# Last units of two products by column halves, and sixteen modulation columns moved

## The chip, the cores and the metric

One NeuronCore of one Trainium2 chip runs the program. The metric is the device time of one execution in microseconds (us); all times here are in us unless marked ns.

## The reference

512 tokens of 1024 channels pass through a first block (a short gated convolution, then a squared-ReLU MLP, both with modulation by a vector c) and through two layers of a second block. What matters for the change is the first block and the step into the second:

```python
mod_lat = [m[:, None, :] for m in jnp.split(jax.nn.silu(c) @ ada_w[i] + ada_b[i], N_MOD, axis=-1)]
g_pre, g_post, g_pre_ff, g_post_ff = norm_gains[i]
a_lat = modulate(rmsnorm(h_lat, g_pre), mod_lat[0], mod_lat[1])
y_lat = short_gated_conv(a_lat, sc_w_in[j], sc_conv[j], sc_w_out[j])
h_lat = h_lat + mod_lat[2] * rmsnorm(y_lat, g_post)
f_lat = squared_relu_mlp(modulate(rmsnorm(h_lat, g_pre_ff), mod_lat[3], mod_lat[4]), mlp_w_in[i], mlp_w_out[i])
h_lat = h_lat + mod_lat[5] * rmsnorm(f_lat, g_post_ff)
...
h = rms_norm(x, even_norm_g[i])
x = x + even_mixer(h, even_w_in[i], ...)
```

An rmsnorm divides each token by the root of its mean square over the 1024 channels.

## The kernel before

**Tiling.** Activations are kept with channels on the partitions: 8 chunks of 128 channels by 512 tokens (X, Y, XH, HH and so on). A matrix product is cut into units of 256 output columns. For a unit, SyncE loads the weights into RAW, ScalarE rounds them to a high half WH (hi_half), VectorE subtracts to get the low half WL (lo_half), and TensorE does three matmuls (high by high, high by low, low by high) for each of 8 chunks of input and each of 2 halves of output, 48 in all. The two output chunks go to PSUM banks 2j and 2j+1, with j = unit % 2. `product` (line 1844) does both halves inside its loop over the input chunks, so both banks are complete only at the unit's end (semaphore s_mm).

**Units.** 0 to 11 are the gated convolution's input product, 12 to 15 its output product, 16 to 47 the MLP (four groups of four units in and four units out), from 48 on the second block.

**Border 1, after unit 15.** The output Y has to be normalised, scaled, added to X, and X normalised again before unit 16 can start. To save a pass over X, the mean square of the new X is put together from three sums over channels: of Y squared (bank S1), of the gated Y squared (S2) and of the cross product 2·gate·Y·X (S3). The loop over units 12 to 15 (VectorE at lines 1427 to 1443, ScalarE at 817 to 826) copies the two chunks of a unit out of PSUM (L1431), makes cross products (L1438), squares (L688) and gated squares (L826), and adds the squares of units 12 to 14 up in SQ (L1163). GpSimd (POOL, lines 566 to 578) adds the cross products and gated squares of chunks 0 to 5 into SQ3 and SQ2. VectorE adds the last pair of each itself (L1445, L1447). TensorE sums over channels with matmuls on a matrix of ones, which are fp32 and appear in the trace as two passes each: last_squares (L1922), SQ2 (L2079), SQ3 (L2082), two_squares (L1928), the last cross products (L2085) and the last gated squares (L2087). Behind them stand the sixteen columns of the MLP's modulation (mod_columns, L1955): one column of PSUM for 128 rows of the modulation, a matmul with 128 weights columns and one moving column, again two passes each; and keep_busy (L1909), matmuls whose result nobody reads. ScalarE takes Ln and Exp of the first sum into R (L696, L698). VectorE then works out the second mean square in four operations (L1464, L1467, L1469, L1472), ScalarE takes its root into SQ (L831, L833), and VectorE and ScalarE make X, its scaled form (L1459), shift it (L703), round it to XH (L706) and subtract to XL (L1485) chunk by chunk. VectorE adds the bias to the columns at L1478 and L1480 in between. Units 16 and 17 are multiplied together, chunk by chunk (two_units).

**Border 2, after unit 47.** The same with one norm fewer: residual_window (L1278) adds the last output chunks to Y, ScalarE squares them, TensorE sums SQ (L1922), three columns, the last two squares (L1928), five columns and three keep_busy matmuls; R follows at L696, and post_norm feeds unit 48.

**What sets the order.** Every engine runs its instructions in the order written, and semaphores tie them. Each POOL addition waits for its product and for the addition before it; cross_product(n) and gated_square(n) have two buffers each, chosen by n % 2.

Of the kernel before, what the change touches and what calls it, by code (L numbers as in the profile page):

```python
# [22 lines left out]
ALU = mybir.AluOpType  # L23
# [4 lines left out]
P = 128  # L28
# [133 lines left out]
def program(nc, i, out):  # L162
    ctx = ExitStack()
    with ctx:
# [5 lines left out]
        def sem(name):  # L170
            return ctx.enter_context(nc.semaphore(name))
# [114 lines left out]
        s_pn, e_g = sem("postnorm_scaled"), sem("logit_scaled")  # L286
        c_z, c_t, c_y, c_g, c_h = (sem("gconv_" + x) for x in ("cv", "centre", "taps", "gated", "hi"))
        m_r, m_f, m_h = (sem("mlp_" + x) for x in ("relu", "squared", "hi"))
# [251 lines left out]
        def _(pool):  # L540
# [24 lines left out]

            for n in range(1, 6):
                pool.wait_ge(x_p, n + 1)
                if n == 1:
                    pool.tensor_tensor(SQ3, cross_product(0), cross_product(1), ALU.add).then_inc(x_sp, 1)
                else:  # L570
                    pool.wait_ge(x_sp, n - 1)
                    pool.tensor_tensor(SQ3, SQ3, cross_product(n), ALU.add).then_inc(x_sp, 1)
                pool.wait_ge(x_q, n + 1)
                if n == 1:
                    pool.tensor_tensor(SQ2, gated_square(0), gated_square(1), ALU.add).then_inc(x_sq, 1)
                else:
                    pool.wait_ge(x_sq, n - 1)
                    pool.tensor_tensor(SQ2, SQ2, gated_square(n), ALU.add).then_inc(x_sq, 1)
# [87 lines left out]
        def _(act):  # L666
# [147 lines left out]
            act.activation(PS_[:, S0_BANK, :], PS_[:, S0_BANK, :], ACT.Exp, scale=-2.0).then_inc(s_ms, 1)  # L814
            for u in range(12, 16):
                if u < 15:
                    hi_half(u + 2, u % 2, 0)
                    hi_half(u + 2, u % 2, 1)
                for c in range(2):
# [323 lines left out]
        def _(dve):  # L1143
# [282 lines left out]
            dve.tensor_scalar(sc_(S_2MG0, 8), sc_(S_MG0, 8), 2.0, None, ALU.mult).then_inc(s_sm, 1)  # L1426
            for u in range(12, 16):
                n0, j, last = 2 * (u - 12), u % 2, u == 15
                dve.wait_ge(s_mm, u + 1)
# [9 lines left out]
                if not last:  # L1439
                    lo_half(u + 2, j, 0)  # L1440
                    lo_half(u + 2, j, 1)
                    add_square(ST_Y0, n0)
                    add_square(ST_Y0, n0 + 1)
# [78 lines left out]
            clear_sum(ST_Y1)  # L1522
            for u in range(U_MLP + 28, U_MLP + 32):
                residual_window(u, u % 2, 2 * (u - U_MLP - 28), ST_Y1, Y)
            post_norm(ST_Y1, 1, S_MG1, "even_norm")
            prep_late(U_EVEN + 1)
# [316 lines left out]
        def _(pe):  # L1843
# [230 lines left out]
            mod_columns(16, 24)  # L2074
            for u in range(12, 16):
                product(u, u % 2, HH, HL, 8, s_h, 0)
            last_squares(ST_Y0, S1_BANK)
            pe.wait_ge(x_sq, 5)
            pe.matmul(PS_[:, S2_BANK, :], ONES[:, :], SQ2, start=True, stop=False)  # L2079
            pe.wait_ge(x_sp, 5)  # L2080
            pe.wait_ge(s_ev, 15)
            pe.matmul(PS_[:, S3_BANK, :], ONES[:, :], SQ3, start=True, stop=False)  # L2082
            two_squares(ST_Y0, S1_BANK)
            pe.wait_ge(x_pair, 1)
            pe.matmul(PS_[:, S3_BANK, :], ONES[:, :], cross_product(6), start=False, stop=True).then_inc(x_23, 1)  # L2085
            pe.wait_ge(x_pair, 2)
            pe.matmul(PS_[:, S2_BANK, :], ONES[:, :], gated_square(6), start=False, stop=True).then_inc(x_23, 1)  # L2087
            pe.wait_ge(s_ad, 16)
            pe.wait_ge(s_sm, 15)
            pe.wait_ge(s_ev, 16)  # L2090
            keep_busy(1, 2)
            mod_columns(24, 32, last=False)
            keep_busy(1, 2)
            mod_columns(32, 40)
            keep_busy(2, 2)
            for g in range(4):
# [422 lines left out]
```

## Time and profile before

| | |
|---|---|
| three runs | 1703.54, 1704.07, 1704.09; median 1704.07 |
| the profiled execution | 1704.55 |
| its span, first to last instruction | 1702.8 |
| TensorE busy | 1685.1 (99% of the span), 7761 matmul records |
| VectorE, ScalarE, GpSimd busy | 1095.9, 692.2, 163.3 |
| mean granted TensorE clock | 0.998 |
| window 213.35 to 232.30 (border 1) | TensorE busy 18.95, granted clock 0.82 |
| window 577 to 600 (border 2) | TensorE busy 21.98, granted clock 1.00 |

The profiled execution's own time is 1.75 above its span. Busy time of TensorE counts keep_busy too, and matmuls overlap in their records: two in a row start 0.227 apart where each shows 0.39.

### The profile page before, as it was taken

To read this page: it belongs to the slowest core of one execution; us is meant where nothing else is said; L and a number is where in the kernel's file an instruction comes from. 1 tells how busy PE (TensorE), PEld (TensorE's weight loads), DVE (VectorE), ACT (ScalarE), POOL (GpSimd) and SP (SyncE) were. 2 spreads that over 40 slices of the span, in tenths; PEclk is the share of its full clock that TensorE was granted. 3 is DMA by queue.
4 is the path that set the end of the run, shared out by engine and by line. 5 is a ranking of instruction groups with operands and counts; after the bars stand their busy time and mean duration, and the time that the engine had idled before them with its cause. 6 is when DMAs were issued, how large, how long until landed. Compare 5 with 4: busy or idle time off the path is not lost.

```text
span 1702.8 us, 21701 instructions
## 1 busy us (share of the span) xinstructions
PE 1685.1 (99%) x7761; PEld 1378.7 (81%) x7761; DVE 1095.9 (64%) x1680; ACT 692.2 (41%) x992; POOL 163.3 (10%) x160
## 2 busy tenths in 40 slices
PE   8999999999999999999999999999999999999999
PEld 7888878888888778888888888888756888888888
DVE  7799885353535586755664664769998666366374
ACT  4322353232323346644432432447666443243243
POOL 1000400000000042100000000005881000000000
PEclk9999999999999999999999999999999999999999
DMA  8676314333332133503323322232211323323222
GB/s 280 219 236 220 129 57 131 99 99 99 117 99 93 56 86 106 134 26 99 123 99 99 123 99 85 78 85 55 70 50 50 99 99 99 99 98 99 79 82 87
DMA packets 184994, 180.46 MB, mean 106 GB/s; under 512 B 3888, under 2 KB 182324, under 8 KB 184924
## 3 DMA queue, kind: packets, MB, share of 16 engines
q1 hardware_dynamic: 184924, 179.54, 33.1%
q8 instruction: 43, 0.70, 0.2%
q14 instruction: 27, 0.22, 0.0%
HBM read 173.15 MB, written 2.10 MB: 103 GB/s over the span
## 4 chain that ended last, share of the span: by engine, by line
PE 88%; DVE 7%; issue 2%; POOL 1%; ACT 1%; DMA 0%; DVEq 0%; POOLq 0%; SPq 0%; ACTq 0%
PE PSUM L1857 23%; PE PSUM L1858 23%; PE PSUM L1859 23%; DVE PSUM L1789 3%; POOL CP L635 1%; PE PSUM L2238 1%; DVE WL L1150 1%; PE PSUM L2270 1%; PE PSUM L2269 1%; PE PSUM L1890 1%; PE PSUM L1891 1%; PE PSUM L1889 1%; PE PSUM L2271 1%; PE PSUM L2303 1%; PE PSUM L2304 1%
## 5 line engine op out<-in xcount | busy, mean ns | idle before, releaser
L675 ACT ACTIVATE WH<-RAW 128x1024 fp32r<-128x1024 f32 x266 | 273.6, 1053 | 711.4 <-PE PSUM L1859 673.0
L1857 PE MATMUL PSUM<-XH,WH 128*128 128x512 f32 x1152 | 449.5, 390 | 0.0
L1858 PE MATMUL PSUM<-XL,WH 128*128 128x512 f32 x1152 | 448.2, 389 | 0.0
L1859 PE MATMUL PSUM<-XH,WL 128*128 128x512 f32 x1152 | 448.2, 389 | 0.0
L1150 DVE TENSOR_TENSOR WL<-RAW,WH 128x1024 fp32r<-128x1024 f32 x270 | 331.0, 1248 | 7.9 <-ACT WH L675 7.7
L1857 PEld LDWEIGHTS PSUM<-XH,WH 128*128 128x128 f32 x1152 | 216.2, 188 | 45.4 <-issue 0.7
L1858 PEld LDWEIGHTS PSUM<-XL,WH 128*128 128x128 f32 x1152 | 216.2, 188 | 45.4 <-issue 0.7
L1859 PEld LDWEIGHTS PSUM<-XH,WL 128*128 128x128 f32 x1152 | 216.2, 188 | 45.2
L1857 PE MATMUL PSUM<-HH,WH 128*128 128x512 f32 x632 | 246.6, 390 | 0.4
L1859 PE MATMUL PSUM<-HH,WL 128*128 128x512 f32 x632 | 246.0, 389 | 0.0
L1858 PE MATMUL PSUM<-HL,WH 128*128 128x512 f32 x632 | 245.9, 389 | 0.0
L1671 DVE TENSOR_TENSOR ZP<-PSUM,R 128x512 f32<-128x512 f32 x88 | 56.7, 687 | 172.1 <-PE PSUM L1859 172.1
L1857 PEld LDWEIGHTS PSUM<-HH,WH 128*128 128x128 f32 x632 | 118.6, 188 | 27.0 <-DVE HL L1695 2.1
L1859 PEld LDWEIGHTS PSUM<-HH,WL 128*128 128x128 f32 x632 | 118.6, 188 | 24.8
L1858 PEld LDWEIGHTS PSUM<-HL,WH 128*128 128x128 f32 x632 | 118.6, 188 | 24.4
L1278 DVE TENSOR_TENSOR X<-PSUM,X 128x512 f32 (+1 forms) x60 | 38.6, 686 | 141.7 <-PE PSUM L1859 110.9
L635 POOL TENSOR_TENSOR CP<-CP,PRD 128x512 f32<-128x512 f32 x67 | 86.3, 1289 | 451.2 <-ACT PRD L1101 431.7
L1682 DVE SCALAR_TENSOR_TENSOR TA<-ZP,VCOL,TA 128x512 f32<-128x512 f32 x176 | 120.2, 747 | 0.0
L1789 DVE SCALAR_TENSOR_TENSOR PSUM<-UPAD,VCOL,PSUM 128x512 f32<-128x512 f32 x123 | 83.4, 749 | 0.4
L1185 DVE SCALAR_TENSOR_TENSOR MACC<-ARAW,small,MACC 128x256 f32<-128x256 f32 x140 | 70.5, 504 | 5.0
L1504 DVE TENSOR_SCALAR TA<-PSUM 128x512 f32<-128x512 f32 x32 | 20.6, 686 | 80.3 <-PE PSUM L1859 78.4
L994 ACT ACTIVATE TA<-ZP,VCOL 128x512 f32<-128x512 f32 x88 | 66.4, 802 | 0.0
(401 smaller groups left out, 2062.4 us busy)
## 6 DMA issues: line engine op xcount, KB each, us to landing
RAW<-in_ffn_w_up SPq DMA_DIRECT2D x44, 1024.0 KB, 5.1
ARAW<-in_ada_w SPq DMA_DIRECT2D x24, 1024.0 KB, 5.3
RAW<-in_mlp_w_in SPq DMA_DIRECT2D x16, 1024.0 KB, 5.3
RAW<-in_mlp_w_out SPq DMA_DIRECT2D x16, 1024.0 KB, 4.9
RAW<-in_ffn_w_down SPq DMA_DIRECT2D x16, 1024.0 KB, 5.0
RAW<-in_sc_w_in SPq DMA_DIRECT2D x9, 1024.0 KB, 5.1
RAW<-in_even_w_in SPq DMA_DIRECT2D x8, 1024.0 KB, 5.6
RAW<-in_ffn_w_down SPq DMA_DIRECT2D x8, 768.0 KB, 4.4
```

The lines of the kernel that those rows point to most:

```text
L635: pool.tensor_tensor(CP[:, n, :], CP[:, n, :], PRD[:, before % RING, :], ALU.add).then_inc(g_a, 1)
L675: act.activation(WH[:, j, a:b, :], RAW[:, j, a:b, :], ACT.Copy).then_inc(s_hi, 1)
L994: act.activation(TA[:, c, :], ZP[:, c, 2:T + 2], ACT.Identity, scale=col(f"fw{layer}2", it * 2 + (half + 2 * first + c)), bias=col(f"fb{la ...
L1150: tt(WL[:, j, a:b, :], RAW[:, j, a:b, :], WH[:, j, a:b, :].bitcast(F32), ALU.subtract).then_inc(s_lo, 1)
L1185: stt(dst, w, s, dst, ALU.mult, ALU.add).then_inc(s_as if k < 7 else s_ad, 1)
L1278: ins = dve.tensor_copy(d, src) if first else tt(d, src, d, ALU.add)
L1671: tt(ZP[:, c, 2:T + 2], banks(j, c), R[:, :], ALU.mult).then_inc(f_z, 1)
L1682: stt(TA[:, c, :], ZP[:, c, tap:tap + T], col(f"fw{layer}{tap}", it * 2 + (half + 2 * first + c)), TA[:, c, :], ALU.mult, ALU.add).then_in ...
L1789: stt(acc, src, w, acc, ALU.mult, ALU.add).then_inc(g_v, 1)
L1857: pe.matmul(o, wh, mh[:, k, :], start=(k == 0), stop=False)
L1858: pe.matmul(o, wh, ml[:, k, :], start=False, stop=False)
L1859: mm = pe.matmul(o, wl, mh[:, k, :], start=False, stop=(k == kn - 1))
```

## The change

At both borders the last unit is multiplied by output halves: all 24 matmuls of the first half, a semaphore, then all 24 of the second. VectorE takes chunk 6 out after the first and chunk 7 after the second, and adds the square of chunk 6 to SQ in between; TensorE then sums SQ and the square of chunk 7 only. At border 1, GpSimd also adds chunk 6's cross product and gated square, VectorE's two pair additions are gone, and the last sums take chunk 7 alone. The sixteen modulation columns move from border 1 to behind units 12 and 13, eight each, and VectorE's two small operations on them to a place in front of chunk 6. VectorE's v1 waits for one of the two last sums rather than both. keep_busy is six in a row at border 1 (before: one, one, two) and two at border 2 (before: three). ScalarE's rounding of the first half of unit 17's weights stands between its work for chunk 6 and chunk 7.

```diff
@@ gpsimd
-            for n in range(1, 6):
+            for n in range(1, 7):
                 pool.wait_ge(x_p, n + 1)
@@ scalar
-            for u in range(12, 16):
-                if u < 15:
-                    hi_half(u + 2, u % 2, 0)
-                    hi_half(u + 2, u % 2, 1)
+            for u in range(12, 15):
+                hi_half(u + 2, u % 2, 0)
+                hi_half(u + 2, u % 2, 1)
...
+            square(ST_Y0, 6, Y[:, 6, :])
+            gate(6)
             hi_half(U_MLP + 1, 1, 0)
+            square(ST_Y0, 7, Y[:, 7, :])
+            gate(7)
             rms(ST_Y0, 1.0 / D, S1_BANK)
@@ vector
-            dve.wait_ge(x_p, 8)
-            tt(cross_product(6), cross_product(6), cross_product(7), ALU.add).then_inc(x_pair, 1)
-            dve.wait_ge(x_q, 8)
-            tt(gated_square(6), gated_square(6), gated_square(7), ALU.add).then_inc(x_pair, 1)
+            def last_chunk(n):
+                dve.tensor_copy(Y[:, n, :], banks(1, n % 2)).then_inc(s_xu, 1)
+                dve.wait_ge(s_xu, 8 * ST_Y0 + n + 1)
+                if n == 7:
+                    dve.tensor_copy(sc_(S_DUMP), sc_(S_EPS)).then_inc(s_ev, 1)
+                dve.wait_ge(x_sp, n - 2)
+                stt(cross_product(n), Y[:, n, :], sc_(S_2MG0 + n), X[:, n, :], ALU.mult, ALU.mult).then_inc(x_p, 1)
+            dve.wait_ge(s_ac, 6)
+            tt(sc_(S_MOD + 24, 16), PS_[:, COL_BANK, 24:40], col("ada_b", 24, 16), ALU.add).then_inc(s_sm, 1)
+            dve.wait_ge(s_sm, 18)
+            stt(sc_(S_GS1, 8), sc_(S_MOD + 32, 8), 1.0, col("gains", 16, 8), ALU.add, ALU.mult).then_inc(s_sm, 1)
+            dve.wait_ge(t_mm, T_MM + 1)
+            last_chunk(6)
+            dve.wait_ge(s_sqr, squares_before(ST_Y0) + 7)
+            dve.wait_ge(s_sqa, sum_steps(ST_Y0) + 7)
+            tt(SQ[:, :], SQ[:, :], TF[:, 0, :], ALU.add).then_inc(t_sqa, 1)
+            dve.wait_ge(s_mm, 16)
+            last_chunk(7)
             lo_half(U_MLP + 1, 1, 0)
...
             dve.wait_ge(s_r, ST_Y0 + 1)
+            dve.wait_ge(x_23, 1)
+            tt(v, PS_[:, S2_BANK, :], R[:, :], ALU.mult).then_inc(x_v, 1)
             dve.wait_ge(x_23, 2)
-            tt(v, PS_[:, S2_BANK, :], R[:, :], ALU.mult).then_inc(x_v, 1)
             gated(0)
...
+            dve.wait_ge(t_mm, T_MM + 2)
+            tt(Y[:, 6, :], banks(1, 0), Y[:, 6, :], ALU.add).then_inc(s_xu, 1)
+            dve.wait_ge(s_sqr, squares_before(ST_Y1) + 7)
+            dve.wait_ge(s_sqa, sum_steps(ST_Y1) + 7)
+            tt(SQ[:, :], SQ[:, :], TF[:, 0, :], ALU.add).then_inc(t_sqa, 1)
+            dve.wait_ge(s_mm, U_MLP + 32)
+            tt(Y[:, 7, :], banks(1, 1), Y[:, 7, :], ALU.add).then_inc(s_xu, 1)
@@ tensor
-            for u in range(12, 16):
+            for u in range(12, 15):
                 product(u, u % 2, HH, HL, 8, s_h, 0)
+                if u == 12:
+                    pe.wait_ge(s_ad, 16)
+                    pe.wait_ge(s_sm, 15)
+                if u < 14:
+                    mod_columns(24 + 8 * (u - 12), 32 + 8 * (u - 12), last=(u == 13))
+            def chunk_by_chunk(u, base_):
+                pe.wait_ge(s_ev, u - 1)
+                for c in range(2):
+                    for k in range(8):
...
+                        pe.matmul(o, wh, HH[:, k, :], start=(k == 0), stop=False)
+                        pe.matmul(o, wh, HL[:, k, :], start=False, stop=False)
+                        mm = pe.matmul(o, wl, HH[:, k, :], start=False, stop=(k == 7))
+                    mm.then_inc(*((t_mm, 1) if c == 0 else (s_mm, 1)))
+            chunk_by_chunk(15, 0)
+            pe.wait_ge(t_sqa, T_SQA + 1)
+            pe.matmul(PS_[:, S1_BANK, :], ONES[:, :], SQ[:, :], start=True, stop=False)
+            pe.wait_ge(x_sp, 6)
+            pe.wait_ge(s_ev, 15)
+            pe.matmul(PS_[:, S3_BANK, :], ONES[:, :], SQ3, start=True, stop=False)
+            pe.wait_ge(s_sqr, squares_before(ST_Y0) + 8)
+            pe.matmul(PS_[:, S1_BANK, :], ONES[:, :], TF[:, 1, :], start=False, stop=True).then_inc(s_ss, 1)
+            pe.wait_ge(x_sq, 6)
+            pe.matmul(PS_[:, S2_BANK, :], ONES[:, :], SQ2, start=True, stop=False)
+            pe.wait_ge(x_q, 8)
+            pe.matmul(PS_[:, S2_BANK, :], ONES[:, :], gated_square(7), start=False, stop=True).then_inc(x_23, 1)
+            pe.wait_ge(x_p, 8)
+            pe.matmul(PS_[:, S3_BANK, :], ONES[:, :], cross_product(7), start=False, stop=True).then_inc(x_23, 1)
             pe.wait_ge(s_ev, 16)
-            keep_busy(1, 2)
-            mod_columns(24, 32, last=False)
-            keep_busy(1, 2)
-            mod_columns(32, 40)
-            keep_busy(2, 2)
+            keep_busy(6, 2)
...
+            for u in range(U_MLP + 28, U_MLP + 31):
+                product(u, u % 2, HH, HL, 8, s_h, 32)
+            chunk_by_chunk(U_MLP + 31, 32)
...
-            last_squares(ST_Y1, ST_BANK)
+            pe.wait_ge(t_sqa, T_SQA + 2)
+            pe.matmul(PS_[:, ST_BANK, :], ONES[:, :], SQ[:, :], start=True, stop=False)
             mod_columns(40, 43, last=False)
-            two_squares(ST_Y1, ST_BANK)
+            pe.wait_ge(s_sqr, squares_before(ST_Y1) + 8)
+            pe.matmul(PS_[:, ST_BANK, :], ONES[:, :], TF[:, 1, :], start=False, stop=True).then_inc(s_ss, 1)
             mod_columns(43, 48)
-            keep_busy(3)
+            keep_busy(2)
```

## Rows read from the trace of the kernel before

**Rows 1.** The page: busy time by engine, and the weights' low halves among the groups
```profile
PE 1685.1 (99%) x7761; PEld 1378.7 (81%) x7761; DVE 1095.9 (64%) x1680; ACT 692.2 (41%) x992; POOL 163.3 (10%) x160
...
L1150 DVE TENSOR_TENSOR WL<-RAW,WH 128x1024 fp32r<-128x1024 f32 x270 | 331.0, 1248 | 7.9 <-ACT WH L675 7.7
```
**Rows 2.** Timeline of VectorE, unit 14's end to unit 15's (start us, us, engine line)
```profile
202.66 1.29 DVE L1431 COPY Y<-PSUM 128x512 f32<-128x512 f32 x2 [0.40 <-PE PSUM L1859]
...
204.06 1.42 DVE L1438 SCALAR_TENSOR_TENSOR ZP<-Y,small,X 128x512 f32<-128x512 f32 x2
205.39 4.35 DVE L1150 TENSOR_TENSOR WL<-RAW,WH 128x1024 fp32r<-128x1024 f32 x2
209.67 3.47 DVE L1163 TENSOR_TENSOR SQ<-SQ,TF 128x512 f32<-128x512 f32 x2
213.55 1.29 DVE L1431 COPY Y<-PSUM 128x512 f32<-128x512 f32 x2 [0.41 <-PE PSUM L1859]
```
**Rows 3.** Timeline of ScalarE at border 1
```profile
214.27 1.23 ACT L688 ACTIVATE TF<-Y 128x512 f32<-128x512 f32 x2 [7.34 <-DVE Y L1431]
...
217.84 0.69 ACT L696 ACTIVATE R<-PSUM,small 128x512 f32<-128x512 f32 x1 [0.17 <-PE PSUM L1928]
...
225.64 0.81 ACT L703 ACTIVATE TF<-TA,small 128x512 f32<-128x512 f32 x1 [1.34 <-DVE small L1480]
```
**Rows 4.** Timeline of TensorE at border 1
```profile
218.50 1.02 PE L2087 MATMUL PSUM<-MACC,ONES 128*128 128x512 f32 x2
...
219.35 1.02 PE L1909 MATMUL PSUM<-VCOL,IDENT 128*128 128x512 f32 x2
...
222.86 2.33 PE L1955 MATMUL PSUM<-ONES,MACC 128*128 128x1 f32 x16
...
227.82 1.42 PE L1869 MATMUL PSUM<-XH,WH 128*128 128x512 f32 x1
...
246.02 0.39 PE L1889 MATMUL PSUM<-XH,WH 128*128 128x512 f32 x1
```
**Rows 5.** Timeline of VectorE at border 1
```profile
219.63 0.69 DVE L1464 TENSOR_TENSOR TF<-PSUM,R 128x512 f32<-128x512 f32 x1 [0.69 <-PE PSUM L2087]
...
220.83 0.68 DVE L1467 TENSOR_TENSOR TF<-PSUM,TF 128x512 f32<-128x512 f32 x1
...
225.22 0.18 DVE L1478 TENSOR_TENSOR small<-PSUM,VCOL 128x16 f32<-128x16 f32 x1 [0.20 <-PE PSUM L1955]
...
244.98 0.69 DVE L1485 TENSOR_TENSOR XL<-TF,XH 128x512 fp32r<-128x512 f32 x1 [0.95 <-ACT XH L706]
```
**Rows 6.** Window of 1 us: length, PE, PEld, DVE, ACT, POOL busy, then clock
```profile
224.00:225.00 1.00, 1.00 (x7) 1.00 (x7) 0.90 (x2) 0.30 (x1) 0.00 (x0) 0.52 0.00 0
```
**Rows 7.** Timelines of TensorE and VectorE: the eight columns behind unit 11
```profile
167.97 1.84 PE L1955 MATMUL PSUM<-ONES,MACC 128*128 128x1 f32 x16
...
168.17 1.29 DVE L1404 TENSOR_TENSOR TA<-PSUM,TA 128x512 f32<-128x512 f32 x2
...
180.90 1.29 DVE L1431 COPY Y<-PSUM 128x512 f32<-128x512 f32 x2 [2.89 <-PE PSUM L1859]
```
**Rows 8.** Timeline at border 2
```profile
570.84 1.48 DVE L1163 TENSOR_TENSOR SQ<-SQ,TF 128x512 f32<-128x512 f32 x2
...
578.06 1.29 DVE L1278 TENSOR_TENSOR Y<-PSUM,Y 128x512 f32<-128x512 f32 x2 [5.74 <-PE PSUM L1859]
...
578.78 1.23 ACT L688 ACTIVATE TF<-Y 128x512 f32<-128x512 f32 x2 [8.55 <-DVE Y L1278]
...
581.49 0.69 ACT L696 ACTIVATE R<-PSUM,small 128x512 f32<-128x512 f32 x1 [1.48 <-PE PSUM L1928]
```
**Rows 9.** Timeline of POOL behind unit 14
```profile
204.90 1.53 POOL L572 TENSOR_TENSOR MACC<-MACC,ZP 128x512 f32<-128x512 f32 x1 [3.19 <-DVE ZP L1438]
...
210.85 1.74 POOL L578 TENSOR_TENSOR MACC<-MACC 128x512 f32<-128x512 f32 x1
```
**Rows 10.** Timeline of TensorE: its longest later wait
```profile
1266.85 5.42 PE L2432 MATMUL PSUM<-UPAD,DG 128*128 128x512 f32 x12 [1.48 <-DVE UPAD L1758]
```

More of the change, by code:

```diff
@@ L286, in program @@
         s_pn, e_g = sem("postnorm_scaled"), sem("logit_scaled")
-        c_z, c_t, c_y, c_g, c_h = (sem("gconv_" + x) for x in ("cv", "centre", "taps", "gated", "hi"))
+        c_z, c_t, c_y, c_g, c_h = (sem("gconv_" + x) for x in ("cv", "centre", "taps", "gated", "hi_then_square_added"))
         m_r, m_f, m_h = (sem("mlp_" + x) for x in ("relu", "squared", "hi"))
@@ L1426, in _ @@
             dve.tensor_scalar(sc_(S_2MG0, 8), sc_(S_MG0, 8), 2.0, None, ALU.mult).then_inc(s_sm, 1)
[L1427 to L1428 removed]
+            for u in range(12, 15):
+                n0, j = 2 * (u - 12), u % 2
                 dve.wait_ge(s_mm, u + 1)
@@ L1438, in _ @@
                     stt(cross_product(n), Y[:, n, :], sc_(S_2MG0 + n), X[:, n, :], ALU.mult, ALU.mult).then_inc(x_p, 1)
[L1439 to L1443, printed above, removed]
-            dve.wait_ge(x_p, 8)
-            tt(cross_product(6), cross_product(6), cross_product(7), ALU.add).then_inc(x_pair, 1)
-            dve.wait_ge(x_q, 8)
-            tt(gated_square(6), gated_square(6), gated_square(7), ALU.add).then_inc(x_pair, 1)
+                lo_half(u + 2, j, 0)
+                lo_half(u + 2, j, 1)
+                add_square(ST_Y0, n0)
+                add_square(ST_Y0, n0 + 1)
+            def last_chunk(n):
[16 more added lines that the diff above has]
+            last_chunk(7)
             lo_half(U_MLP + 1, 1, 0)
@@ L1522, in _ @@
             clear_sum(ST_Y1)
-            for u in range(U_MLP + 28, U_MLP + 32):
+            for u in range(U_MLP + 28, U_MLP + 31):
                 residual_window(u, u % 2, 2 * (u - U_MLP - 28), ST_Y1, Y)
+            dve.wait_ge(t_mm, T_MM + 2)
[5 more added lines that the diff above has]
+            tt(Y[:, 7, :], banks(1, 1), Y[:, 7, :], ALU.add).then_inc(s_xu, 1)
+            dve.wait_ge(s_xu, 8 * ST_Y1 + 8)
+            dve.tensor_copy(sc_(S_DUMP), sc_(S_EPS)).then_inc(s_ev, 1)
             post_norm(ST_Y1, 1, S_MG1, "even_norm")
@@ L2074, in _ @@
             mod_columns(16, 24)
-            for u in range(12, 16):
+            for u in range(12, 15):
                 product(u, u % 2, HH, HL, 8, s_h, 0)
[L2077 to L2080, printed above, removed]
+                if u == 12:
[3 more added lines that the diff above has]
+                    mod_columns(24 + 8 * (u - 12), 32 + 8 * (u - 12), last=(u == 13))
@@ new lines, in chunk_by_chunk @@
+            def chunk_by_chunk(u, base_):
+                pe.wait_ge(s_ev, u - 1)
+                for c in range(2):
+                    for k in range(8):
+                        if c == 0:
+                            if k % 4 == 0:
+                                pe.wait_ge(s_lo, halves(u, k // 4 + 1))
+                            pe.wait_ge(s_h, base_ + k + 1)
+                        wh, wl = (w[:, 1, k, c * P:c * P + P] for w in (WH, WL))
+                        o = PS_[:, 2 + c, :]
+                        pe.matmul(o, wh, HH[:, k, :], start=(k == 0), stop=False)
+                        pe.matmul(o, wh, HL[:, k, :], start=False, stop=False)
+                        mm = pe.matmul(o, wl, HH[:, k, :], start=False, stop=(k == 7))
+                    mm.then_inc(*((t_mm, 1) if c == 0 else (s_mm, 1)))
@@ L2102, in _ @@
                     x_units(U_MLP + 8 * g, 4, 8)
-                h_units(U_MLP + 8 * g + 4, 4, 8 + 8 * g)
+                if g < 3:
+                    h_units(U_MLP + 8 * g + 4, 4, 8 + 8 * g)
+            for u in range(U_MLP + 28, U_MLP + 31):
+                product(u, u % 2, HH, HL, 8, s_h, 32)
+            chunk_by_chunk(U_MLP + 31, 32)
             pe.wait_ge(s_ad, 20)
```

25 lines of the change are left out of this document (9 added, 16 removed).

## The prediction

> **What bounds the kernel now.** I read the page's busy table first: TensorE is busy for 1685.1 of 1702.8 us [rows 1], so whatever is put into its stream costs its full length, and whatever leaves it helps only where it was not waiting there. Next I read the windows of 1 us and the timelines of the two places that the diff names, the end of unit 15 (border 1) and the end of unit 47 (border 2). At both, TensorE runs statistics and filler while VectorE and ScalarE prepare its next input.
>
> Border 1 starts when VectorE first copies from unit 15's banks, at 213.55 [rows 2]. I count from there and call it E. The chain is: copies, squares on ScalarE, sums over channels on TensorE, Ln of the first sum at 217.84, which is E+4.3 [rows 3]; the gated sum (L2087) fills TensorE's slot from 218.50, the next matmul starts at 219.35, and VectorE's first product of the second norm (v1, L1464) starts at 219.63, E+6.1 [rows 4, 5]. So one ONES matmul takes 0.86, and its reader starts 0.27 after the slot ends. v2 (L1467) starts at 220.83, E+7.3. The chain then meets the modulation columns: VectorE has nothing to do from 225.02, waits 0.20 for them and spends 0.3 on two small operations [rows 5]; TensorE spent its 222.86 to 225.05 on the second block of them [rows 4]. In 224 to 225 the granted clock is 0.52 [rows 6], that is the 1.2 GHz level, after 32 narrow column passes with little between; filler and first matmuls run at half rate, and the first real matmul is at 227.82, E+14.3, and shows 1.42 where others show 0.39 [rows 4]. Yet what ends this border is not that: VectorE feeds XL chunk by chunk, its last chunk (L1485 at 244.98, done 245.67) is used by TensorE at 246.02 [rows 4, 5], a slack of only 0.35.
>
> **The change, part by part.**
>
> (1) Sixteen columns move into the stream, in two blocks of eight, behind units 12 and 13. A block of eight is already in the stream behind unit 11: its sixteen passes are busy for 1.84 [rows 7], and from unit 11's end (VectorE at 168.17) to unit 12's (180.90) pass 12.73, against 10.89 for a unit without a block (202.66 to 213.55) [rows 2, 7], which gives 1.84 again. Both are a bit long by rounding and pipeline fill; I take 1.8 each, **+3.6**. Nothing hides it, since TensorE has no wait there. Bounds: 1.7 (the next unit's first matmul pulled in) and 2.2 (the block of 222.86 to 225.05) each. Its waits are free: the sums of MACC they need are finished before unit 12. The two small VectorE operations, 0.3, go in front of chunk 6.
>
> (2) Border 1, chunk by chunk. Chunk 6's matmuls end half a unit, 24 x 0.227 (10.89 by 48) = 5.4, before E, but is VectorE there to take it? Its queue behind unit 14 is: two copies and two products from 202.66, two WL halves of 4.35 from 205.39, two adds of 3.47 from 209.67, the end at 213.14, E-0.4 [rows 2]. One WL half alone takes 1.25 [rows 1] and two adds alone 1.48 [rows 8], so 3.9 of this is waiting, at the time of POOL's four adds (204.90 to 212.59) [rows 9]: about one POOL add, 1.0 to 1.15, for each VectorE operation. The diff changes none of this work and puts chunk 6 behind it. So **chunk 6 is taken up at about E-0.1, not at E-5.4**, and in place of two copies in a row there is now copy, product, add, copy:
> - VectorE: copy 6 to 0.6, cross product 6 (0.71 each [rows 2]) to 1.4, ScalarE's square 6 (0.62 [rows 3]) ready at 1.25, add to SQ 1.3 to 2.0, copy 7 to 2.65.
> - POOL, which now also sums n=6: cross add held until 2.0, done 3.15; cross product 7 then 3.15 to 3.85; POOL's gated add 3.85 to 5.0.
> - TensorE, in the order of the new code: SQ 2.1 to 2.95; SQ3 (needs POOL's 3.15) 3.25 to 4.1; square 7 to 4.95, so Ln at 5.2 where it was 4.3; SQ2 (needs POOL's 5.0) 5.05 to 5.9; gated square 7 to 6.75; cross product 7 to 7.6.
> - VectorE: v1 at 7.0 (was 6.1), Y chunk 0 at 7.9, v2 at 8.5 (was 7.3): +1.2.
>
> From v2 on the work is the same, less the wait and the small operations: ScalarE's first split, at 225.64 [rows 3], could start at 225.04, -0.6. The chain is 0.6 later. TensorE, with no columns and its clock kept, uses up the slack of 0.35 less a 0.05 wake-up: border 1 costs **+0.3**. What the restored clock gives elsewhere is cut off by VectorE's feed.
>
> (3) Border 2. No POOL work here, and unit 46's adds end at 572.32 [rows 8], before chunk 6 of unit 47 ends (578.06-5.4=572.6), so it really is taken early. Before, the squares of both chunks take ScalarE from 578.78 to 580.01, and Ln starts at 581.49 [rows 8]. After, square 7 is ready at 579.4, TensorE has SQ (0.86) and three columns (0.7) until 579.4, then one ONES matmul in place of two: Ln at 580.5. **-1.0**, and all of it carries on, since the next unit is fed by this chain. One filler less costs nothing: TensorE still ends filler before its input.
>
> (4) Order of matmuls inside units 15 and 47, new semaphores, one more POOL round, the dump copy: no cost. Both units' inputs and WL are ready long before, and POOL's next task is at unit 47's end. No DMA is moved; SP's loads wait for WL halves whose time shifts by about 1 us, and they have far more than that in hand.
>
> **Sum:** 3.6 + 0.3 - 1.0 = +2.9. The profiled execution took 1704.55 (span 1702.8, 1.75 around it) and would take 1707.45; it stands 0.48 above the median of 1704.07, so I forecast **1707.0**. That is 0.17%; about 0.2%, 3.4 us, is what a measurement here can tell from no change.
>
> **A rule against the trace.** Who gets in first at E+1.4, VectorE's add or POOL's cross add, is settled in my sum by 0.15: the add has its square at 1.3, POOL sees the product at 1.4 and starts about 0.1 later (204.06+0.71=204.77, then 204.90) [rows 2, 9]. The Trainium skill (SBUF — State Buffer, Who interferes with whom) states that a VectorE instruction with two SBUF inputs and a GpSimd instruction reading SBUF exclude each other for a whole instruction, the first to start winning. By that rule the order is worth a POOL add; if the two merely shared time, the sum would be some 0.5 more than mine.
>
> **Rivals.**
> - **POOL gets in first** at E+1.4. The add to SQ then ends at 3.3 in place of 2.0, and TensorE's six matmuls start at 3.4 and run without the two waits: the last ends 8.55, not 7.6. +0.95, sum +3.9, **1708.0**. For: the margin is only 0.15. Against: ScalarE's square is quick and VectorE goes straight from one operation to the next.
> - **The clock falls in the new gap** (slower). TensorE waits from E-0.2 to 2.1, then in smaller pieces. Against: it waited 1.48 in one go before 1266.85 [rows 10] with no fall, since border 1 accounts for all the clock that the trace lost: 0.18 of its window of 18.95 is 3.4, and so is 0.002 of the span. For: the only fall in this trace is at this border [rows 6], after narrow passes that filled 1.84+2.2 us. It decides once the level drops before E+6.75: with the six matmuls at half rate from about 5, the last 2.6 us take 5.2. Sum +5.5, **1709.6**. The Trainium skill (TensorE: Matmul & The Clock Gate, What's actually happening) says that activity holds the gate open and idleness closes it; this gap is new idleness, so the rule speaks for this rival.
> - **Chunk 6 is taken early at border 1 after all**, if VectorE's queue is shorter than measured. Without its lag v1 comes at about 4.95 and v2 at 6.4, the chain is 1.5 earlier and the border 1.8 shorter: 3.6-1.8-1.0=+0.8, **1704.9**. Against: 213.14. Even this is not faster, as the columns eat it.
> - **The columns are free in the stream**: sum -0.7, **1703.4**. Against: the 1.84 measured twice [rows 7]. To be faster by 3.4 both of the last two must hold (-2.8) and more.
>
> **How the numbers follow.** Forecast 0.60, POOL first 0.15, clock falls 0.10, chunk 6 early 0.08, free columns 0.03, both or something unseen on the fast side 0.04. The forecast's own spread, mostly columns at 1.7 to 2.2, is 1706.2 to 1707.9; a quarter of it lies over 1707.5. Slower: 0.15+0.15+0.10=0.40. Faster 0.04. Same 0.56. The range goes from the chunk-early case less 0.2 to the clock case plus 0.2: 1704.7 to 1709.8.
>
> **What would show it.** Unit ends 12 to 13 and 13 to 14 about 12.7 apart; the copy of chunk 6 not before 0.2 ahead of unit 15's last matmul; a TensorE gap of some 2.3 there; Ln about 5.2 and v2 about 8.5 after that matmul; no row with clock 0.5; Ln of border 2 at 2.5 (was 3.4) after unit 47's end. Copy 6 some 4 to 5 us before E would break step 2; unit distances near 10.9 would break step 1.

## The result, and the profile after

| | before | changed |
|---|---|---|
| executions | 14 | 14 |
| median | 1703.91 | 1707.13 |
| lowest and highest | 1703.06 and 1704.52 | 1706.74 and 1709.31 |
| profiled execution, its span | 1704.55, 1702.8 | 1707.69, 1705.9 |

The ratio is 1.0022, interval 1.0015 to 1.0029: a small loss, 3.2 us between the medians, right at the 0.2% that a measurement here can tell. The forecast was 1707.0.

The page's busy table of the changed kernel does not show where they come from. TensorE is busy for 2.2 us less than before [rows 1] in a span 3.1 longer; at border 1 it now waits where it ran slowly before:
```profile
PE 1682.9 (99%) x7759; PEld 1376.2 (81%) x7759; DVE 1097.8 (64%) x1680; ACT 692.0 (41%) x992; POOL 165.0 (10%) x162
```
The timelines show where the time went. First VectorE from unit 11's end to border 1 (start us, us, engine line; in brackets the idle time before and what ended it):
```profile
168.49 1.29 DVE L1414 TENSOR_TENSOR TA<-PSUM,TA 128x512 f32<-128x512 f32 x2
...
181.21 1.29 DVE L1441 COPY Y<-PSUM 128x512 f32<-128x512 f32 x2 [2.89 <-PE PSUM L1891]
...
193.94 1.29 DVE L1441 COPY Y<-PSUM 128x512 f32<-128x512 f32 x2 [4.27 <-PE PSUM L1891]
...
206.67 1.29 DVE L1441 COPY Y<-PSUM 128x512 f32<-128x512 f32 x2 [2.26 <-PE PSUM L1891]
...
213.67 3.47 DVE L1173 TENSOR_TENSOR SQ<-SQ,TF 128x512 f32<-128x512 f32 x2
...
217.35 0.68 DVE L1456 COPY Y<-PSUM 128x512 f32<-128x512 f32 x1
...
218.74 0.68 DVE L1471 TENSOR_TENSOR SQ<-SQ,TF 128x512 f32<-128x512 f32 x1
...
224.23 0.69 DVE L1490 TENSOR_TENSOR TF<-PSUM,R 128x512 f32<-128x512 f32 x1 [1.10 <-PE PSUM L2141]
...
225.63 0.68 DVE L1494 TENSOR_TENSOR TF<-PSUM,TF 128x512 f32<-128x512 f32 x1
...
249.26 0.69 DVE L1508 TENSOR_TENSOR XL<-TF,XH 128x512 fp32r<-128x512 f32 x1 [0.95 <-ACT XH L709]
251.72 1.29 DVE L1527 TENSOR_SCALAR TA<-PSUM 128x512 f32<-128x512 f32 x2 [1.76 <-PE PSUM L1923]
```
The ends of units 12 to 14 lie 12.73 and 12.73 apart where a unit without columns takes 10.89: 3.68 for both blocks. Adding one plain unit to the last end gives unit 15's end, E, as 206.67 + 10.89 = 217.56. No copy can be seen there, because chunk 6 is taken up only at 217.35, 0.2 ahead of E, behind the additions of L1173 that end at 217.14. From here on all times of border 1 are given behind E.

Next POOL, ScalarE and TensorE at border 1, in this order:
```profile
218.90 1.47 POOL L575 TENSOR_TENSOR MACC<-MACC,ZP 128x512 f32<-128x512 f32 x1 [2.31 <-DVE ZP L1461]
...
222.45 0.69 ACT L699 ACTIVATE R<-PSUM,small 128x512 f32<-128x512 f32 x1 [1.05 <-PE PSUM L2137]
...
219.48 1.12 PE L2132 MATMUL PSUM<-SQ,ONES 128*128 128x512 f32 x2 [1.97 <-DVE SQ L1471]
220.44 1.11 PE L2135 MATMUL PSUM<-MACC,ONES 128*128 128x512 f32 x2
...
231.49 0.47 PE L1901 MATMUL PSUM<-XH,WH 128*128 128x512 f32 x1 [1.36 <-issue]
```
| behind E | before | predicted | changed |
|---|---|---|---|
| chunk 6 taken up | 0.0 | -0.1 | -0.2 |
| SQ summed (L2132) | | 2.1 | 1.9 |
| Ln | 4.3 | 5.2 | 4.9 |
| v1 | 6.1 | 7.0 | 6.7 |
| v2 | 7.3 | 8.5 | 8.1 |
| last XL chunk | 31.4 | | 31.7 |
| unit 16's end | 34.03 | +0.3 | 34.16 |

The border's length is taken to the first reader of unit 16 (251.72 - 217.56 = 34.16). In the kernel before that reader stood here in VectorE's timeline:
```profile
247.58 1.29 DVE L1504 TENSOR_SCALAR TA<-PSUM 128x512 f32<-128x512 f32 x2 [1.91 <-PE PSUM L1891]
```
247.58 - 213.55 [rows 2] = 34.03, so border 1 costs 0.13 between these two profiles. They differ in the clock too: the run of border 2 by itself, below, shows that 0.13 is 0.58 from the edit less 0.45 from a fall of the clock that the changed kernel's profile does not have.

At border 2, VectorE and ScalarE of the changed kernel:
```profile
576.78 0.69 DVE L1549 TENSOR_TENSOR Y<-PSUM,Y 128x512 f32<-128x512 f32 x1 [0.30 <-PE PSUM L2127]
...
582.22 0.69 DVE L1554 TENSOR_TENSOR Y<-PSUM,Y 128x512 f32<-128x512 f32 x1 [3.36 <-PE PSUM L2127]
...
584.79 0.69 ACT L699 ACTIVATE R<-PSUM,small 128x512 f32<-128x512 f32 x1 [1.22 <-PE PSUM L2165]
```
Chunk 6 is taken up 5.4 ahead of chunk 7, and Ln follows the unit's end by 2.57, where it was 581.49 - 578.06 = 3.43 [rows 8]: -0.86. It carries on: unit 48's first matmul starts 6.61 behind the unit's end, where it was 7.47. The three terms give 3.68 + 0.13 - 0.86 = +2.95. The profiled executions differ by 3.14. The remaining 0.19 is not put down to the change: 0.32 is there before its first instruction (unit 11's end at 168.49, was 168.17 [rows 7]), and some of it is lost again later.

### The profile page after: what moved, and what is told of

The parts are those of the page before. It is cut to its first block, busy times and chain, and to the rows that moved or that the text cites. A ratio compares the mean times of both kernels' runs of the same rounds, so it can differ in the third digit from the quotient of the medians.

```text
span 1705.9 us, 21687 instructions
## 1 busy us (share of the span) xinstructions
PE 1682.9 (99%) x7759; PEld 1376.2 (81%) x7759; DVE 1097.8 (64%) x1680; ACT 692.0 (41%) x992; POOL 165.0 (10%) x162
## 4 chain that ended last, share of the span: by engine, by line
PE 86%; DVE 9%; issue 2%; ACT 1%; POOL 1%; DMA 0%; DVEq 0%; POOLq 0%; SPq 0%; ACTq 0%
PE PSUM L1889 23%; PE PSUM L1890 23%; PE PSUM L1891 23%; DVE PSUM L1821 3%; DVE WL L1160 1%; POOL CP L638 1%; PE PSUM L2294 1%; PE PSUM L2326 1%; PE PSUM L2325 1%; PE PSUM L2327 1%; PE PSUM L1921 1%; PE PSUM L1922 1%; PE PSUM L2359 1%; PE PSUM L1923 1%; PE PSUM L2360 1%
## 5 line engine op out<-in xcount | busy, mean ns | idle before, releaser
L1889 PE MATMUL PSUM<-HH,WH 128*128 128x512 f32 x600 | 234.4, 391 | 0.4
L1891 PE MATMUL PSUM<-HH,WL 128*128 128x512 f32 x600 | 233.5, 389 | 0.0
L1890 PE MATMUL PSUM<-HL,WH 128*128 128x512 f32 x600 | 233.5, 389 | 0.0
L1889 PEld LDWEIGHTS PSUM<-HH,WH 128*128 128x128 f32 x600 | 112.6, 188 | 25.7 <-DVE HL L1727 2.1
L1891 PEld LDWEIGHTS PSUM<-HH,WL 128*128 128x128 f32 x600 | 112.6, 188 | 23.6
L1890 PEld LDWEIGHTS PSUM<-HL,WH 128*128 128x128 f32 x600 | 112.6, 188 | 23.1
```

The costliest lines, as they stand in the source:

```text
L1889: pe.matmul(o, wh, mh[:, k, :], start=(k == 0), stop=False)
L1890: pe.matmul(o, wh, ml[:, k, :], start=False, stop=False)
L1891: mm = pe.matmul(o, wl, mh[:, k, :], start=False, stop=(k == kn - 1))
```

## The experiments

The kernel before ran again beside each group of experiments: its median was 1703.42 beside the first four, 1704.01 beside the next three, and 1703.91 beside the changed kernel. A difference to the changed kernel's 1707.13 is one between groups, and can be some 0.5 off; where that matters, the traces decide.

**Border 2 by itself**, on the kernel before. The edit is the diff of border 2 shown above and nothing else:
```diff
-            for u in range(U_MLP + 28, U_MLP + 32):
+            for u in range(U_MLP + 28, U_MLP + 31):
                 residual_window(u, u % 2, 2 * (u - U_MLP - 28), ST_Y1, Y)
+            dve.wait_ge(t_mm, T_MM + 1)
...
-            last_squares(ST_Y1, ST_BANK)
+            pe.wait_ge(t_sqa, T_SQA + 1)
+            pe.matmul(PS_[:, ST_BANK, :], ONES[:, :], SQ[:, :], start=True, stop=False)
...
-            keep_busy(3)
+            keep_busy(2)
```


> The kernel before with border 2 alone changed (unit 47 by output halves, its chunk 6 squared and added early, three to two fillers). My theory: the Ln after unit 47 starts 2.6 us after VectorE takes chunk 7, where it was 3.4, everything behind it follows, and the kernel takes 0.9 us less than before (ratio 0.9995). Rival, that the changed kernel's border 2 gave nothing that lasts: ratio 1.0000. Border 1 keeps its fall of the clock (granted mean 0.998) in both.

Measured: 1702.73 against 1703.42, ratio 0.9995 (0.9986 to 1.0004). The interval takes in 1, so the times alone don't show a gain; the trace shows the mechanism. Chunk 7's addition on VectorE and Ln on ScalarE:
```profile
577.10 0.69 DVE L1534 TENSOR_TENSOR Y<-PSUM,Y 128x512 f32<-128x512 f32 x1 [3.36 <-PE PSUM L2100]
...
579.67 0.69 ACT L699 ACTIVATE R<-PSUM,small 128x512 f32<-128x512 f32 x1 [1.22 <-PE PSUM L2143]
```
The distance is 2.57 again, 0.86 less than before, and the median fell by 0.7.

This profile also holds border 1, which the edit leaves as it was, with a shorter fall of the clock. VectorE's rows are the first copy behind unit 15, the first of the two small operations and the first reader of unit 16; the windows have the granted clock behind the five busy times:
```profile
213.04 1.29 DVE L1434 COPY Y<-PSUM 128x512 f32<-128x512 f32 x2 [0.41 <-PE PSUM L1871]
...
224.43 0.17 DVE L1481 TENSOR_TENSOR small<-PSUM,VCOL 128x16 f32<-128x16 f32 x1
...
246.62 1.29 DVE L1507 TENSOR_SCALAR TA<-PSUM 128x512 f32<-128x512 f32 x2 [1.75 <-PE PSUM L1903]
```
```profile
224.00:225.00 1.00, 1.00 (x4) 0.49 (x4) 0.97 (x4) 0.17 (x1) 0.00 (x0) 0.59 0.00 0
...
227.00:228.00 1.00, 1.00 (x3) 0.42 (x2) 0.96 (x3) 0.66 (x2) 0.00 (x0) 0.71 0.00 0
```
In the kernel before the fall went on from 224 [rows 6] into this window:
```profile
230.00:231.00 1.00, 1.00 (x4) 0.80 (x3) 1.00 (x3) 0.53 (x1) 0.00 (x0) 0.56 0.00 0
```
The border takes 246.62 - 213.04 = 33.58 here and took 34.03 there, with the same instructions: the long fall cost 0.45. Of it, 0.28 is there at the small operation (E+11.39 against E+11.67 [rows 5]), which waits for the second block of columns, 1.84 long here and 2.33 there. So against a border with the short fall the change's border 1 costs 34.16 - 33.58 = 0.58, and only the end of the long fall brings that down to 0.13. The times agree: the executions of the kernel before with a granted clock of 0.998 (8 of 33 and 11 of 27) have medians 0.6 and 0.7 over the others. That this difference comes from border 1 alone is not shown.

**The columns by themselves**, on the kernel before:
```diff
                 product(u, u % 2, HH, HL, 8, s_h, 0)
...
+                if u < 14:
+                    mod_columns(24 + 8 * (u - 12), 32 + 8 * (u - 12), last=(u == 13))
...
-            keep_busy(1, 2)
-            mod_columns(24, 32, last=False)
-            keep_busy(1, 2)
-            mod_columns(32, 40)
-            keep_busy(2, 2)
+            keep_busy(6, 2)
```


> The kernel before with the sixteen columns alone moved behind units 12 and 13, six fillers in a row at border 1, VectorE's two small operations where they were. My theory: units 13 and 14 end 12.73 us after the unit before them in place of 10.88, +3.7 us in all, and border 1 gives back at most 0.5 (a wait of 0.2 gone, and the slack of 0.35 at the last chunk used up because the clock stays up): +3.1 to +3.5 us, ratio 1.0019. Rival, that narrow columns in the stream cost no more than at the border: about 0. Second rival, that the clock kept up is worth its whole 3.4 us of lost clock: ratio 1.0000 to 1.0002.

Measured: 1707.67 (1706.95 to 1707.87) against 1703.42, ratio 1.0023 (1.0014 to 1.0032). VectorE's timeline, the ends of units 12 to 14 and of unit 16:
```profile
180.28 1.29 DVE L1431 COPY Y<-PSUM 128x512 f32<-128x512 f32 x2 [2.89 <-PE PSUM L1859]
...
193.01 1.29 DVE L1431 COPY Y<-PSUM 128x512 f32<-128x512 f32 x2 [4.27 <-PE PSUM L1859]
...
205.73 1.29 DVE L1431 COPY Y<-PSUM 128x512 f32<-128x512 f32 x2 [2.26 <-PE PSUM L1859]
...
250.19 1.29 DVE L1504 TENSOR_SCALAR TA<-PSUM 128x512 f32<-128x512 f32 x2 [1.75 <-PE PSUM L1891]
```
The same 12.73 and 12.72. The border is 250.19 - (205.73 + 10.89) = 33.57, that is 0.46 less than in the profile of the kernel before, and the same as the 33.58 of the run before this one. So the columns and their two small operations had cost nothing at the border, the long fall of the clock had cost the half microsecond, and in the stream the columns cost 3.7. That is +3.2 by the trace against the border with the long fall and +3.7 against the one with the short fall; this profiled execution, 1707.02, is 3.6 over the median of before. But most of the eleven executions lie 0.7 higher than it, and the median at +4.25, which I had not expected. The clock does not part the two groups: of the three near 1707.0 two have 1.000 and one 0.999, of the eight near 1707.7 three have 1.000 and five 0.999. The last run goes into that and doesn't settle it.

**Two fillers in the new wait**, on the changed kernel, after chunk_by_chunk(15, 0):
```diff
+            keep_busy(2, 7)
             pe.wait_ge(t_sqa, T_SQA + 1)
```


> The changed kernel with two fillers (1.72 us) put in TensorE's gap of 2.0 us behind unit 15. The changed kernel's executions fall in two groups, 9 at 1706.7 to 1707.7 with a granted clock of 1.000 and 5 at 1708.5 to 1709.3 with 0.999. Theory: the second group is the clock falling at border 1 because of that gap; with the gap filled no execution shows 0.999, and all lie within 1706.5 to 1707.3, in the median as the first group. Rival, that the 0.999 comes from elsewhere (the idle stretch of 1.36 us ahead of unit 16, or another place): the second group stays, about one in three. Rival, that the fillers hold up the first sum: the Ln comes up to 0.1 us later, no more.

Measured: 1706.92 (1706.69 to 1707.15), ratio 1.0019 (1.0010 to 1.0028). TensorE's timeline has the wait nearly closed:
```profile
216.59 1.88 PE L1941 MATMUL PSUM<-VCOL,IDENT 128*128 128x512 f32 x4
218.71 1.12 PE L2133 MATMUL PSUM<-SQ,ONES 128*128 128x512 f32 x2 [0.25 <-DVE SQ L1471]
```
The border stays at 34.16 (unit 15's end 216.79, unit 16's 250.95) and Ln at 4.9: TensorE's emptiness there is no cost by itself. What does change is the spread. All eleven executions have a granted clock of 1.000, while of the 14 of the changed kernel five had 0.999, and these are its slowest, 1708.48 to 1709.31; the other nine lie between 1706.74 and 1707.69. Two profiles further below go into that. Against its own kernel before, this one is 3.50 slower and the changed kernel 3.22, so no gain of the median is shown.

**POOL's additions cut to 8 of 512 tokens**, on the changed kernel, with the sums taken from chunks 6 and 7 alone:
```diff
-                    pool.tensor_tensor(SQ3, SQ3, cross_product(n), ALU.add).then_inc(x_sp, 1)
+                    pool.tensor_tensor(SQ3[:, 0:8], SQ3[:, 0:8], cross_product(n)[:, 0:8], ALU.add).then_inc(x_sp, 1)
...
-            pe.matmul(PS_[:, S3_BANK, :], ONES[:, :], SQ3, start=True, stop=False)
+            pe.matmul(PS_[:, S3_BANK, :], ONES[:, :], cross_product(6), start=True, stop=False)
```


> The changed kernel with GpSimd's twelve additions done on 8 of 512 columns, and the two sums over channels taken from chunk 6's products alone, so the cross and gated sums of chunks 0 to 5 are left out; every other instruction and wait stays. Theory: it was GpSimd's additions that held VectorE up behind unit 14 (one of them for each VectorE operation with two SBUF inputs); without them VectorE is free about 4.2 us ahead of unit 15's end in place of 0.2, takes chunk 6 then, the Ln starts about 3.1 us after unit 15's end (4.9 in the changed kernel), the second VectorE product about 5.8 (8.1), and the kernel takes 2.0 to 2.6 us less than the changed one: about +0.8 us against before, ratio 1.0005. Rival, that chunk 6 is late for another reason, such as VectorE's own work: no difference against the changed kernel, ratio 1.0019.

Measured: 1704.87 (1704.51 to 1705.62), ratio 1.0007 (0.9998 to 1.0016), 2.26 below the changed kernel, or 1.8 when each is taken against its own kernel before. VectorE's timeline:
```profile
210.97 1.48 DVE L1173 TENSOR_TENSOR SQ<-SQ,TF 128x512 f32<-128x512 f32 x2
...
212.66 0.68 DVE L1456 COPY Y<-PSUM 128x512 f32<-128x512 f32 x1
...
216.83 0.69 DVE L1456 COPY Y<-PSUM 128x512 f32<-128x512 f32 x1 [2.10 <-PE PSUM L2127]
...
222.81 0.68 DVE L1494 TENSOR_TENSOR TF<-PSUM,TF 128x512 f32<-128x512 f32 x1
```
The two additions of L1173 take 1.48 in place of 3.47, chunk 6 is taken up 4.2 ahead of E (216.83 here) and v2 follows at 6.0 in place of 8.1. The border falls to 248.87 - 216.83 = 32.04, by 2.1, which accounts for the gain. So taking chunk 6 early does work at border 1, and POOL's additions are what took it away. By the Trainium skill (SBUF — State Buffer, Who interferes with whom) a VectorE instruction with two SBUF inputs and a GpSimd instruction that reads SBUF exclude each other; this pair of runs agrees, with 3.47 against 1.48 for the same two additions.

**Eight columns in the wait, eight behind the last sum**, on the changed kernel, with the two small operations back behind scaled(0):
```diff
-                if u < 14:
-                    mod_columns(24 + 8 * (u - 12), 32 + 8 * (u - 12), last=(u == 13))
...
             chunk_by_chunk(15, 0)
...
+            mod_columns(24, 32, last=False)
             pe.wait_ge(t_sqa, T_SQA + 1)
...
-            keep_busy(6, 2)
+            mod_columns(32, 40)
+            keep_busy(4, 2)
```


> The changed kernel with the sixteen columns out of the stream: eight in TensorE's gap behind unit 15 (1.8 us of columns in 2.0 us of waiting), eight behind the last sum in place of two fillers, VectorE's two small operations back at their old place. Theory: units 13 and 14 are again 10.88 apart, -3.7; the 0.3 of the small operations only moves from ahead of chunk 6 to behind the second root; so 3.7 less than the changed kernel, 0.5 less than before, ratio 0.9997. Rival, that columns in the gap hold up the sum of SQ or let the clock fall: the first sum's Ln later than 4.9 after unit 15's end, or a granted clock of 0.999 and up to 2 us lost, ratio 1.0005 or more.

Measured: 1703.21 (1703.05 to 1703.8) against 1704.01, ratio 0.9996 (0.9987 to 1.0005), 3.9 below the changed kernel. In TensorE's timeline a block fits the wait, and the first sum starts behind it without a wait of its own:
```profile
212.94 1.84 PE L1987 MATMUL PSUM<-ONES,MACC 128*128 128x1 f32 x16
214.78 1.13 PE L2130 MATMUL PSUM<-SQ,ONES 128*128 128x512 f32 x2
```
The border is 34.09 (unit 14's end at 202.26, unit 16's at 247.24), so all sixteen columns are free here, and the 3.7 was the price of their place. One block takes time in which TensorE waited, the other takes the place of filler.

**One low half of unit 16's weights behind chunk 7**, on the changed kernel:
```diff
-                lo_half(u + 2, j, 1)
+                if u < 14:
+                    lo_half(u + 2, j, 1)
...
             last_chunk(7)
+            lo_half(U_MLP, 0, 1)
             lo_half(U_MLP + 1, 1, 0)
```


> The changed kernel with VectorE's second half of unit 16's low weights moved from behind unit 14 to behind chunk 7. Theory: VectorE's queue decides, so chunk 6 is taken 2.0 to 2.2 us ahead of unit 15's end in place of 0.2; the Ln comes at about 3.2 us after it (4.9), the first VectorE product is then held by the moved work until 5.1 to 5.4 (6.7), the second at 6.5 to 6.7 (8.1): 1.3 to 1.6 us less than the changed kernel, ratio 1.0011 against before. Rival, that the work only changes its place and the border stays DVE-bound: 0 to 0.3 less, ratio 1.0018.

Measured: 1705.62 (1705.42 to 1706.5), ratio 1.0011 (1.0002 to 1.0020), 1.5 below the changed kernel (1.6 with each against its own kernel before). VectorE's timeline, and one row of POOL's:
```profile
214.19 1.06 DVE L1467 SCALAR_TENSOR_TENSOR small<-small,VCOL 128x8 f32<-128x8 f32 x1
215.17 0.68 DVE L1457 COPY Y<-PSUM 128x512 f32<-128x512 f32 x1
...
213.49 1.73 POOL L581 TENSOR_TENSOR MACC<-MACC 128x512 f32<-128x512 f32 x1
```
The time came as expected, but chunk 6 did not move as far: it is taken up at 1.55 ahead of E (216.72). In front of it, the small operation on eight columns took 1.06 where it takes 0.17 in the changed kernel, and it ends at 215.25, when POOL's gated addition does (213.49 + 1.73 = 215.22). So this operation on 128 x 8 values was held until POOL's addition had ended. The border is 249.52 - 216.72 = 32.80, 1.4 less than in the changed kernel. The next run has the small operations in another place.

**Both together, the columns at the border.** The low half stays late, the columns go behind the last sum with one filler between, the small operations behind scaled(0):
```diff
-                if u < 14:
-                    mod_columns(24 + 8 * (u - 12), 32 + 8 * (u - 12), last=(u == 13))
...
-            keep_busy(6, 2)
...
+            mod_columns(24, 32, last=False)
+            keep_busy(1, 2)
+            mod_columns(32, 40)
+            keep_busy(2, 2)
```


> The same with the sixteen columns out of the stream, behind the last sum of border 1 with one filler between the two blocks, and VectorE's small operations at their old place. If both theories hold (columns in the stream cost 3.7, VectorE's queue decides when the border's sums start) it takes 3.7 less than the kernel with the late weights alone and beats both kernels: 1.3 to 1.9 us less than before, ratio 0.9990. If the clock falls as in the kernel before, the loss is at most the slack of 0.35 us.

Measured: 1701.43 (1701.29 to 1702.09) against 1704.01, ratio 0.9987 (0.9978 to 0.9996): the only kernel here whose interval lies wholly below 1. VectorE's timeline:
```profile
210.47 0.68 DVE L1457 COPY Y<-PSUM 128x512 f32<-128x512 f32 x1
...
213.18 0.69 DVE L1457 COPY Y<-PSUM 128x512 f32<-128x512 f32 x1 [0.33 <-PE PSUM L2124]
...
219.16 0.68 DVE L1492 TENSOR_TENSOR TF<-PSUM,TF 128x512 f32<-128x512 f32 x1
...
245.47 1.29 DVE L1529 TENSOR_SCALAR TA<-PSUM 128x512 f32<-128x512 f32 x2 [1.76 <-PE PSUM L1925]
```
Chunk 6 is now 2.7 ahead of E (213.18), v2 at 6.0, and the border 245.47 - 213.18 = 32.29. Against the profile of the kernel before, 32.29 - 34.03 - 0.86 = -2.6, and the medians differ by 2.58. Against the border with the short fall it is 32.29 - 33.58 - 0.86 = -2.15.

**The changed kernel profiled again, twice**, to find where executions with a granted clock of 0.999 lose it.

> The changed kernel once more, for a profile of an execution that shows 0.999 (5 of 14 did, at 1708.5 to 1709.3, against 1706.7 to 1707.7 for 1.000). Theory: such an execution has the 1.2 GHz level in a stretch of border 1, behind TensorE's 2.0 us of waiting, and its sums over channels take 1.7 us each in place of 0.86. Rival: the level falls elsewhere. With 1.000 again, the place stays open.

> The changed kernel a third time, with the same theory (the level falls at border 1, behind the wait of 2.0 us) and the same rival (it falls elsewhere); with 1.000 again the place stays open.

Both came out at 0.999, with 1708.42 and 1708.57. TensorE and ScalarE in the second profile:
```profile
218.49 1.88 PE L2132 MATMUL PSUM<-SQ,ONES 128*128 128x512 f32 x2 [1.97 <-DVE SQ L1471]
220.16 1.92 PE L2135 MATMUL PSUM<-MACC,ONES 128*128 128x512 f32 x2
221.87 1.16 PE L2137 MATMUL PSUM<-TF,ONES 128*128 128x512 f32 x2
...
223.07 0.69 ACT L699 ACTIVATE R<-PSUM,small 128x512 f32<-128x512 f32 x1 [2.67 <-PE PSUM L2137]
```
Its windows of 1 us (length, busy time of PE, PEld, DVE, ACT and POOL, then the granted clock):
```profile
219.00:220.00 1.00, 1.00 (x2) 0.29 (x1) 0.96 (x4) 1.00 (x3) 1.00 (x2) 0.50 0.00 0
220.00:221.00 1.00, 1.00 (x2) 0.34 (x1) 1.00 (x1) 0.40 (x1) 1.00 (x1) 0.50 0.00 0
```
In the first profile the same sums took 1.12, 1.11 and 1.02 at a granted clock of 1.00. Here the level is 1.2 GHz through the first two sums, 3.4 us, behind the wait of 1.97, and Ln comes 4.58 after SQ's sum starts where it came 2.97 after it: +1.6. Unit 16's reader starts at 252.33 with chunk 6 taken up at 216.36, a border of 35.8. The third profile has the fall at the same place, one sum later, over those of L2135 and L2137. Seven of the sixteen executions of the changed kernel have the clock of 0.999, and the two of them with a profile show this.

**The columns by themselves, profiled again**, for the 0.7 left open above.

> The kernel with the moved columns alone once more. Its executions were 1706.95 to 1707.02 (3 of 11, one of them profiled) and 1707.6 to 1707.9 (8 of 11). For a profile of the second kind: theory, a fall of the clock behind one of the column blocks in the stream or at border 1 lengthens it by 0.7; rival, the clock is 1.00 throughout border and blocks, and the 0.7 comes from elsewhere in the kernel.

It took 1707.26 with a granted clock of 0.999, and its fall stands in another place, behind the wait for the border's first input. A row of TensorE's timeline and a window:
```profile
230.10 0.47 PE L1869 MATMUL PSUM<-XH,WH 128*128 128x512 f32 x1 [2.25 <-issue]
```
```profile
231.00:232.00 1.00, 1.00 (x4) 0.81 (x3) 0.96 (x2) 0.39 (x1) 0.00 (x0) 0.50 0.06 16
```
TensorE waits for XL soon again there, so the fall costs almost nothing: the border is 250.32 - 216.73 = 33.59, against 33.57. The 0.7 of the other executions is not explained by it and stays open. It leaves the order of the terms as it is: by every reading, traces and medians, moving the columns costs 3.2 to 4.3.

## Why the prediction was right

The numbers of its steps against the traces:

- **The columns, +3.6: 3.68.** Nothing covers them in the stream. Moved alone they cost about what the whole change does or more, and given a place at the border they cost nothing (34.09 against 34.16 for the border without them, 33.58 against 33.57 in the code before).
- **Chunk 6 at E - 0.1: E - 0.2.** This step decided the sign, as half the diff is there to take chunk 6 early at border 1 and VectorE's queue doesn't let it. Taking POOL out moved the copy to E - 4.2 and gave 2.1; taking one low half out of the queue, with the columns' small operations, moved it to E - 2.7.
- **POOL's cross addition against VectorE's addition to SQ, a margin of 0.15: 0.16** (218.90 against 218.74). The rival in which POOL gets in first did not come about in any of the three profiles of the changed kernel: VectorE's addition took 0.68 or 0.69 each time.
- **Ln 5.2, v1 7.0, v2 8.5: 4.9, 6.7, 8.1.** Each is 0.2 to 0.4 early: copies and additions follow each other in VectorE closer than I had them, so that SQ's sum began at 1.9. The border's +0.3 was a chain 0.6 later, less 0.3 of slack used up. The traces have the last XL chunk 0.27 later (31.70 against 31.43) and only 0.14 less from its end to unit 16's (1.77 against 1.91): +0.13. This is the smallest of the terms and the one that was mis-sized most.
- **The slack at the feed.** In the kernel before, the clock's fall looked like the cost of border 1, and the change removes it, with a granted clock of 1.00 through the whole border in the first profile. The step said that VectorE's feed cuts off what this gives back. That holds for most of it: 3.4 us of clock were lost in the trace, by the prediction's own count, and 0.45 of it reached the end of unit 16, as the unchanged border with the short fall shows (33.58 against 34.03). The step had this smaller and in other places: it did not see that the half clock lengthened the second block of columns, for which VectorE's chain waits. For the rest TensorE only waits longer, 1.97 and 1.36.
- **Border 2, -1.0: -0.86.** The next unit's first matmul has all of it (6.61 against 7.47).
- **The clock falls in the new wait, a chance of 0.10.** This rival is real, and its chance and price are what I had wrong. The text asked for no row with a clock of 0.5; the first profile has none, the two later ones have. It happens in 7 of 16 executions. Two things in the step failed. The evidence against it, a wait of 1.48 before 1266.85 without a fall [rows 10], was a shorter wait and a single profile; what was needed was the clock of several executions. And its price, 2.6 on top of +2.9, was taken over the last three sums, from E+5 on; the level fell at the first or second sum and was back after two: 1708.6 in place of 1709.6 for the median of the five, 1.7 above that of the nine without it (1706.90). The median of 1707.13 lies within the range of the nine, so the forecast holds for the likelier case. With filler in the wait, none of 11 executions shows the case.

The mechanism came out as written in the main, but that the number lies within 0.1 is partly luck. The three terms missed by +0.08, -0.17 and +0.14, which nearly cancel. And 1707.0 was built on a median of 1704.07 from three executions; the fourteen give 1703.91, so that the measured difference of 3.22 is 0.3 more than the +2.9 of the sum, about what the five executions with the fall add to the median of the nine (0.23).

## What to carry to other kernels

Before splitting a unit so that its first half can be taken up early, look at what the taking engine has queued up to that time: here the half was ready 5.4 early and was taken 0.2 early, until another engine's additions or one queued operation was out of the way. Small work belongs in a place where its engine already waits or runs filler. A dip of the clock in such a place is hardly a reason to move it: here the long one cost 0.45 and moving the work 3.7, since in a stream without waits it costs its full length. For a new wait on TensorE, look at the granted clock of many executions and not of one profile, and fill the wait if it comes down in some.

## What was not expected of the hardware

A wait of 1.97 us on TensorE is followed by about 3.4 us at the 1.2 GHz level in some executions of one and the same program and not in others (7 of 16 have a granted clock of 0.999, and the two of these with a profile show it), and a wait of 2.25 likewise in one of two profiles; with the wait filled to 0.25, none of 11 executions show it. And an operation of VectorE on 128 x 8 values, 0.17 by itself, took 1.06 beside a POOL addition of 1.73 and ended with it, in the one profile that has the two together: how small the instruction is did not shorten what it waited.
